# The modulation product of a two-block kernel, on TensorE or on VectorE, and its latent projections in quarters

## The reference

```python
def second_block(x, c, ctx, c_ctx, w_mod, b_mod, ...):
    mod   = silu(c) @ w_mod + b_mod              # w_mod: 1024 x 6144
    sh1, sc1, g1, sh2, sc2, g2 = split(mod, 6)
    mod_c = silu(c_ctx) @ w_mod + b_mod          # only csh1, csc1 are used
    h  = rmsnorm(x, norm1_g) * (1 + sc1) + sh1
    hc = rmsnorm(ctx, norm1_g) * (1 + csc1) + csh1
    qkv, z, ba, sc_p, fn_u = split(h @ w_in)     # latent projections
    ...                                          # the same for hc
    o_ctx, o_lat = bidirectional_gated_delta(context, latent)
    y_dn = (rmsnorm(o_lat) * silu(z)) @ w_dn_out
    y_sc = (sb * conv(sc * sx)) @ w_sc_out
    y_fn = real(fft2(fn_u)) @ w_fn_out
    gates = sigmoid(h @ w_gate + b_gate)         # three of 1024 columns
    merged = gates[0] * y_dn + gates[1] * y_sc + gates[2] * y_fn
    x = x + g1 * (merged @ w_o)
    x = x + g2 * swiglu(rmsnorm(x, norm2_g) * (1 + sc2) + sh2)
    return rmsnorm(x, final_g)
```

## Time and profile before

| | us |
|---|---|
| median of three runs | 1279.43 |
| profiled execution, span from first to last instruction | 1276.8 |
| runs, lowest and highest | 1279.11, 1280.48 |
| TensorE busy | 1239.6 |
| VectorE busy | 861.0 |
| ScalarE busy | 642.9 |
| GpSimd busy | 96.6 |

### The profile page before, as it was taken

One profiled execution on the slowest core, in us unless ns is written; L12 is line 12 of the kernel. 1 busy time (PEld: TensorE's weight loads), 2 busy tenths in 40 slices (PEclk: granted clock), 3 DMA queues, 4 the chain that ended last, 5 costly groups with the idle time before them and its releaser, 6 DMA issues.

```text
span 1276.8 us, 20625 instructions
## 1 busy us (share of the span) xinstructions
PE 1239.6 (97%) x8338; PEld 1101.1 (86%) x8338; DVE 861.0 (67%) x1278; ACT 642.9 (50%) x983; POOL 96.6 (8%) x84
## 2 busy tenths in 40 slices
PE   8999999999999999999999999999899999999997
PEld 7989778888999889999999989986789998888885
DVE  6877656667879278665546866785476776666665
ACT  6574424435666366554463665552345555344443
POOL 0420000000024020000000000324100000000000
PEclk9999999999999999999999999999999999999999
DMA  9635876555673454454443655537115566555530
GB/s 325 205 106 175 282 259 206 195 181 191 223 218 100 136 162 131 136 163 135 163 133 126 195 175 158 173 100 249 48 67 169 194 217 219 203 188 196 198 133 33
DMA packets 164620, 219.15 MB, mean 172 GB/s; under 512 B 5456, under 2 KB 135342, under 8 KB 164398
## 3 DMA queue, kind: packets, MB, share of 16 engines
q1 hardware_dynamic: 162802, 214.45, 51.4%
q10 hardware_dynamic: 1724, 3.39, 0.7%
HBM read 215.99 MB, written 1.05 MB: 170 GB/s over the span
## 4 chain that ended last, share of the span: by engine, by line
PE 85%; DVE 8%; ACT 3%; DVEq 2%; issue 1%; ACTq 1%; DMA 0%
PE bank L555 16%; PE bank L557 16%; PE bank L556 16%; PE bank L599 15%; PE bank L601 7%; DVE w_lo L546 2%; PE bank L645 2%; PE bank L911 1%; PE bank L899 1%; PE bank L1486 1%; PE bank L1465 1%; PE bank L928 1%; DVE arena L1275 1%; PE bank L1689 1%; PE bank L919 1%
## 5 line engine op out<-in xcount | busy, mean ns | idle before, releaser
L546 DVE TENSOR_TENSOR w_lo<-w_raw,w_hi 128x1024 fp32r<-128x1024 f32 (+1 forms) x350 | 421.7, 1249 | 64.8 <-ACT w_hi L537 54.9
L537 ACT ACTIVATE w_hi<-w_raw 128x1024 fp32r<-128x1024 f32 (+1 forms) x350 | 348.8, 1040 | 121.0 <-PE bank L557 62.7
L599 PE MATMUL bank<-act_parts,w_hi 128*128 128x512 f32 x800 | 283.1, 397 | 2.1 <-DVE act_parts L2259 0.7
L555 PE MATMUL bank<-act_parts,w_hi 128*128 128x256 f32 x944 | 271.0, 287 | 6.6 <-DVE act_parts L2344 3.6
L556 PE MATMUL bank<-act_parts,w_hi 128*128 128x256 f32 x944 | 267.0, 283 | 0.0
L557 PE MATMUL bank<-act_parts,w_lo 128*128 128x256 f32 x944 | 266.9, 283 | 0.0
L601 PE MATMUL bank<-act_parts,w_lo 128*128 128x256 f32 x800 | 224.0, 280 | 0.0
L555 PEld LDWEIGHTS bank<-act_parts,w_hi 128*128 128x128 f32 x944 | 180.8, 192 | 14.5 <-issue 8.9
L599 PEld LDWEIGHTS bank<-act_parts,w_hi 128*128 128x128 f32 x800 | 150.1, 188 | 43.5 <-issue 5.8
L556 PEld LDWEIGHTS bank<-act_parts,w_hi 128*128 128x128 f32 x944 | 181.0, 192 | 0.3 <-issue 0.2
L557 PEld LDWEIGHTS bank<-act_parts,w_lo 128*128 128x128 f32 x944 | 181.0, 192 | 0.0
(11 more groups left out here) (340 smaller groups left out, 1583.1 us busy)
## 6 DMA issues: line engine op xcount, KB each, us to landing
w_raw<-in_w_in SPq DMA_DIRECT2D x39, 1024.0 KB, 6.0
w_raw<-in_w_up SPq DMA_DIRECT2D x32, 1024.0 KB, 5.6
w_raw<-in_w_down SPq DMA_DIRECT2D x32, 1024.0 KB, 5.4
w_raw<-in_w_mod SPq DMA_DIRECT2D x24, 1024.0 KB, 5.4
w_raw<-in_w_ffn_in SPq DMA_DIRECT2D x22, 1024.0 KB, 5.2
w_raw<-in_w_gate SPq DMA_DIRECT2D x20, 1024.0 KB, 5.2
w_raw<-in_w_ffn_out SPq DMA_DIRECT2D x11, 1024.0 KB, 5.9
w_raw<-in_w_out SPq DMA_DIRECT2D x8, 1024.0 KB, 5.1
```

Source lines behind the costliest of these rows:

```text
L537: nc.scalar.activation(whi[:, slot, 0:n], raw[:, st.slot(name), n * half:n * (half + 1)], ACT.Copy).then_inc(hi_ready, 1)
L546: nc.vector.tensor_tensor(wlo[:, slot, 0:n], raw[:, st.slot(name), n * half:n * (half + 1)], whi[:, slot, 0:n].bitcast(F32), ALU.subtract) ...
L555: nc.tensor.matmul(o, ahi, bhi, start=start, stop=False, skip_group_check=True)
L599: nc.tensor.matmul(pair(two_banks[m]), whi[:, slot, at:at + P], xall[:, f, :, :], start=f == 0, stop=False, skip_group_check=True)
```

## The change

The modulation chunk is now 256 rows by 1024 columns; six groups of 1024 columns have four parts each, the same 24 MB. VectorE scales each weight row by the condition's value on that partition and adds it to an accumulator of 128 x 1024: two halves a part, for one condition (groups 2 to 5) or two (0 and 1). Behind the fourth part TensorE sums the accumulator over its partitions with a matrix of ones, ScalarE copies the rows, TensorE turns them and VectorE adds the bias. The slot of a part comes free when VectorE has read it. The parts of groups 0 and 1 stand in layer 0's FFN, 2 and 3 in layer 1's, 4 in the gates, 5 in the SwiGLU.

The latent projections are issued in four units of 12 matmuls: 8 units at `ba`, 8 at `norm`, 3 at each T, and 12 in the levels. Their order changes (the Fourier inputs first, z last), `final_norm` comes in the first T with it, the last copy stands behind the levels, and the fills have two banks of their own. The up products of layer 0 stay wide.

```diff
-        "lat": dict(ba=2, norm=4, T0=1, T1=1, T2=1, T3=1, end=1)}
+        "lat": dict(ba=8, norm=8, T0=3, T1=3, T2=3, T3=3, x0=1, z1=1, x1=1, z2=1, x2=1, z3=1, x3=1, z4=1, x4=1, z5=1,
+                    x5=1, z6=1, end=1)}
-LAT_FILL = ["z0", "z1"] + [f"sc{c}" for c in range(6)] + ["fn0", "fn1"]
-LAT_EXTRA = {"P": [("mod", 8)], "x0": [("mod", 9), ("modr", 4)], "z1": [("modc", 4)],
...
+LAT_FILL = ["fn0", "fn1"] + [f"sc{c}" for c in range(6)] + ["z0", "z1"]
+LAT_EXTRA = {"z5": [("fold", 0)], "z6": [("fold", 1)]}
...
+mod_group(0, 0, (16, 18, 21, 24), 27, 28)
+mod_group(0, 1, (30, 33, 36, 39), 43, 44)
+mod_group(1, 2, (19, 21, 23, 25), 27, 28)
+mod_group(1, 3, (30, 32, 34, 36), 37, 38)
+GATE_MODS = {5: 0, 7: 1, 9: 2, 12: 3}
+GATE_SUMMED, GATE_TURNED = 14, 15
+FFN_MODS = {1: 0, 2: 1, 3: 2, 4: 3}
+FFN_SUMMED, FFN_TURNED = 6, 7
...
-        mod_cond = sb("silu_c_cols", [P, KT, 32])
+        mod_cond = sb("silu_c_cols", [P, KT, 2])
+        mod_acc = sb("mod_terms", [P, D])
...
-                mm.then_inc(pieces_done, 1)
+                    if m == ms - 1:
+                        mm.then_inc(pieces_done, 1)
+                    yield
...
+            def mod_rows_sum(g, take):
+
+                b = banks.claim(pe, f"mod{g}", take())
+                pe.wait_ge(S("mod_done"), MOD_PARTS * (g + 1))
+                for c, acc in enumerate((mod_acc[:, :], ctx_acc) if g < CTX_GROUPS else (mod_acc[:, :],)):
+                    for i in range(4):
+                        mm = nc.tensor.matmul(ps[b][32 * i:32 * (i + 1), T * c:T * (c + 1)], ones[:, 0:32],
+                                              acc[:, T * i:T * (i + 1)], start=True, stop=True, skip_group_check=True)
+                mm.then_inc(S("mod_summed"), 1)
...
+            def mod_terms(i):
+
+                g, r = divmod(i, MOD_PARTS)
+                name = ("mod", i)
+                if r == 0 and g:
+                    dve.wait_ge(S("mod_summed"), g)
+                dve.wait_ge(landed[st.slot(name)], st.loads(name))
+                sums = (mod_acc[:, :], ctx_acc) if g < CTX_GROUPS else (mod_acc[:, :],)
+                for half in range(2):
+                    k, w = 2 * r + half, raw[:, st.slot(name), D * half:D * (half + 1)]
+                    for j, acc in enumerate(sums):
+                        if k == 0:
+                            v.tensor_scalar(acc, w, mod_cond[:, k, j:j + 1], None, ALU.mult)
+                        else:
+                            v.scalar_tensor_tensor(acc, w, mod_cond[:, k, j:j + 1], acc, ALU.mult, ALU.add)
+                    if half == 0:
+                        dve.drain()
+                dve.drain().then_inc(S("mod_done"), 1)
...
+                elif before in st.mods:
+                    sp.wait_ge(S("mod_done"), st.mods[before] + 1)
```

More of the change, by code:

```diff
@@ L58 @@
 PW = CH // 2
[L60 to L61 removed]
+MOD_GROUPS = 6
+MOD_ROWS = 256
+MOD_PARTS = D // MOD_ROWS
+CTX_GROUPS = 2
 LAYER_CHUNKS = 52
@@ L271, in attention_order, with mod_group @@
             V(3) + T(4, 5) + conv[2] + ctx[3] + V(4, 5) + conv[3])
-def mod(*chunks):
-    return [("mod", i) for i in chunks]
 FFN_EXTRA = ({}, {})
[L280 to L283, removed]
+def mod_group(layer, g, steps, summed, turned):
+    for r, at in enumerate(steps):
+        FFN_EXTRA[layer].setdefault(at, []).append(("mod", MOD_PARTS * g + r))
+    FFN_EXTRA[layer].setdefault(summed, []).append(("modr", g))
+    FFN_EXTRA[layer].setdefault(turned, []).append(("modc", g))
+mod_group(0, 0, (16, 18, 21, 24), 27, 28)
[6 more added lines that the diff above has]
+FFN_SUMMED, FFN_TURNED = 6, 7
 ATT = [attention_order(layer) for layer in range(DEPTH)]
@@ L562, in project, with project_parts @@
         def project(pe, name, out_tile, kts, act_hi, act_lo, wait_act=None, first=True, last=True):
+            for _ in project_parts(pe, name, out_tile, kts, act_hi, act_lo, wait_act, first, last):
+                pass
+        def project_parts(pe, name, out_tile, kts, act_hi, act_lo, wait_act=None, first=True, last=True):
             n = st.width(name)
@@ L1031, in act_delta @@
                     nc.scalar.activation(rs, rs, ACT.Exp, scale=-0.5).then_inc(S("dn_rs"), 1)
-                fill("norm", 1)
+                fill("norm", FILL[part]["norm"] // (4 if lat else 2))
             fill("norm")
@@ L1113, in act_delta @@
                 fill(f"t{lv}")
+            fill("end")
             for g in range(4):
@@ L1191, in dve_delta @@
                     S("lat_qn" if lat and i < 2 else "dn_kn"), 1)
-                fill("norm", 1)
+                fill("norm", FILL[part]["norm"] // nq)
             fill("norm")
@@ L1545, in first_input @@
                 def first_input(f):
-                    if layer and f == 4:
-                        mod_chunk(12, low)
-                        mod_chunk(13, low)
                     wait("n1_act", f + 1, KT)
@@ L1746, in _, with gate_mods @@
                 full(mm, b)
+            def gate_mods():
+                if l - GATES_AT == GATE_SUMMED:
+                    mod_rows_sum(4, take)
+                if l - GATES_AT == GATE_TURNED:
+                    mod_columns(4)
             for n in range(3):
@@ L2111, in lat_fill @@
             def lat_fill():
-                i = left[0]
+                i, part = divmod(left[0], UNITS)
                 left[0] += 1
-                if i < len(LAT_FILL):
-                    nxt(n_tiles + i)
-                if i and i - 1 not in settled:
+                if i < len(LAT_FILL) and part % 2 == 0:
+                    split_hi(act, ("post", n_tiles + i + 1), (part // 2,))
+                if i and part == 0 and i - 1 not in settled:
                     lat_copy(i - 1)
@@ L2627, in lat_fill @@
             def lat_fill():
-                i = left[0]
+                i, part = divmod(left[0], UNITS)
                 left[0] += 1
-                nxt(n_tiles + i)
+                if part % 2 == 0:
+                    split_lo(dve, ("post", n_tiles + i + 1), (part // 2,))
+                if part:
+                    return
                 if i == 4:
```

223 lines of the change are left out of this document (96 added, 127 removed).

## The result

The changed kernel took 1321.05 us, the median of four runs (1320.04 to 1323.68); the kernel before 1279.95 beside it. The ratio is 1.0322, 95% interval 1.0308 to 1.0337: slower by 41 us, where 12.7 were forecast. The direction was right, the size was off by a factor of three, and the time lies far outside the range.

The account below looks back on a forecast made before the run. TensorE was taken to bound the kernel, with VectorE costing only where a split comes late. The terms summed to +12.7 us on the 1276.8 span, 1289.5, plus 2.6 to the median: 1292.2 us, range 1277 to 1303.

Parts of the forecast that it names:

- part 1: Layer 0's FFN, groups 0 and 1: VectorE's parts delay splits, stalls 23.5, sums and turns 2.8, less 13.4 of modulation: +12.9 us.
- part 2: Modulation chunks TensorE did while waiting: removal brings nothing, only uncovered turns go; layer 1's start -0.9 us.
- part 3: Layer 1's FFN, groups 2 and 3: parts fit VectorE's idle time; sums, turns and 0.3 of stall: +2.0 us.
- latent inputs: First latent input: the hidden modulation chunks' removal brings nothing, their uncovered turn goes: -0.35 us.
- part 4: Latent delta: norm stage -11.8, T stage -1.6, levels with projection quarters +8.4: -5.0 us.
- part 5: Gates, group 4: stalls of 2.2 at the fourth part, 0.65, 0.3 and 0, sum and turn 0.8: +4.0 us.
- w_o: w_o's first chunk: the hidden modulation chunks' removal brings nothing, their uncovered turn goes: -0.36 us.
- part 6: Last FFN, group 5: no stall, +0.8 for sum and turn, -0.35 for the turn that goes: +0.45 us.
- rival C: Three 4.3 us TensorE stalls drop the clock to 1.2 GHz for the next product, 5.6 each: +17, 1309; chance 0.06.
- the stage longer by 13: Sign in layer 0's FFN: the stage from step 14 to 45 grows by 13 us.
- a granted clock below 1 behind a stall: Sign that the forecast is wrong: the clock drops behind a TensorE stall; expected chance of that case 0.06.

Follow-up runs that it names:

- fit_only: Changed kernel with spare matmuls fitted into TensorE's waits, none at the first gate products or in the context's delta: 1309.1 us, ratio 1.0238.
- warm_hidden: Changed kernel with 13 spare matmuls in each of the four places where modulation chunks stood ahead of a TensorE wait: 1320.1 us, ratio 1.0307.
- bank_fix: Changed kernel with group 3's sum of columns ahead of VectorE's split, and group 5's turn and sum a product earlier: 1314.1 us, ratio 1.0271.
- whole_proj: Changed kernel with the ten latent projections whole again at their old places, none in the levels: 1320.7 us, ratio 1.0313.

## Why the prediction was wrong, point by point

The terms, forecast and measured on the two profiled executions (their spans differ by 45.1, as this one was the slowest of its four runs; the medians by 41.1):

| term | forecast | measured | of it slow clock |
|---|---|---|---|
| part 1, layer 0's FFN | +12.9 | +22.9 | 7.8 |
| part 2, layer 1's start | -0.9 | +2.0, with layer 0's gate | 3.3 |
| part 3, layer 1's FFN | +2.0 | +5.6 | 0 here |
| latent inputs | -0.35 | +0.4 | 1.7 |
| part 4, latent delta | -5.0 | -4.1 | about 3 |
| part 5, gates, to w_o's first chunk | +4.0 | +8.6 | 3.3 |
| w_o | -0.36 | -0.5 | 0 |
| part 6, last FFN | +0.45 | +8.1 | 3.3 |
| ahead of layer 0's FFN | 0 | +1.1 | 0 |
| last norm, end | 0 | +0.9 | not counted |

The last column is an estimate: half of each slow stretch, less what of it was idle. It sums to 22, while fit_only, with 41.0 of the 47.8 us of slow stretches gone, gained 12.0 in the medians (15.6 between the profiled executions). So take the column as an upper bound; why a slow stretch costs less than TensorE loses in it is open.

- **Part 1's mechanism was right to the step.** Stalls forecast and measured: 0.6 and 0.6, 2.6 and 2.4, 1.2 and 1.2, 1.0 and 0.7, then 4.3 and 4.47 to 4.48 three times, 1.3 + 0.55 and 1.83 or 1.5 + 0.3; 23.5 in sum against 22.8 (at step 30 0.5 and 0.3 for a forecast of 1.0). One outer bound was added up wrong, 38.2 for 37.2; nothing hangs on it. The terms' price held (1.28 each, 1.2 start to start; a first term 0.75), and so did the sums (8 matmuls and 2 turns as forecast). Missing were the clock and refill, 2 to 3 us by my estimate: a down product behind a stall took 5.7 from start to start at full clock, where an undisturbed one takes 5.48.
- **The step that failed is the clock.** The sum put what TensorE does after a wait at nothing; rival C had it with a chance of 0.06, only behind the three stalls of 4.3, at +17. I had looked at the one wait of 2.77 at the end of the kernel before and taken it as a bound below which nothing happens; right behind it the kernel ends, so it could not show what comes after. The trace of the kernel before does show the lower clock, at both of its ends. TensorE's last matmul ends at 1272.85, and the granted clock falls at 1275.86, in this row (columns as above):

```profile
1274.00:1276.00 2.00, 0.00 (x0) 0.00 (x0) 0.00 (x0) 0.00 (x0) 0.00 (x0) 0.97 0.99 383
```

  At the start, behind a first wait of 3.83 us (longer than the 2.77 that the prediction calls the longest) and one of 1.06, TensorE's matmuls of 256 columns take 0.41 us, as in the slow stretches, and 0.28 from 16.41 on:

```profile
16.02 0.41 PE L555 MATMUL bank<-side_hi,w_hi 128*128 128x256 f32 x1
16.24 0.34 PE L556 MATMUL bank<-side_lo,w_hi 128*128 128x256 f32 x1
16.41 0.28 PE L557 MATMUL bank<-side_hi,w_lo 128*128 128x256 f32 x1
```

  The page's 9 in the first slice hides this, because the record of the clock begins only at 16.3 us; "the granted clock stayed 1.00 in every slice" was a misreading. Behind each of the three stalls the loss was 1.6 to 2.9 and not 5.6, but slow stretches stood behind much shorter waits as well, at nine other places. By fit_only all this is worth 12 of the 28 us between forecast and measurement.
- **"So their removal brings nothing" (part 2) was right about the wait and wrong about the work.** The hidden chunks had cost nothing and kept TensorE from being idle. That removing them costs something is read from the slow stretches behind three of the four places; warm_hidden didn't settle it. Of all the terms of the sum this is the one whose sign a reader would least suspect.
- **Part 6 and part 3: a bank.** I costed the sum and the turn by their own durations and said nothing of the bank that they hold. The ring has four, a wide product takes two, and the bank of the modulation comes up again at the second claim. By bank_fix this is worth 7 us.
- **Part 4 came out at its number for another reason than its working gave it.** whole_proj shows that the quarters brought nothing. What the stage gained is then, as far as the rows say, the eight modulation chunks of 1.06 and their turns that left it, less some 3 us of slow clock; no run took these apart.
- **Part 5**: the fourth part's stall was 2.73 for a forecast of 2.2, with 6.8 us at 1.2 GHz about it.

Of the signs to look for nearly all came: the stalls at 23, 35 and 41, those of 1 to 2 at 26 and 38, the first T at 815.6 in the old time, levels of 9 us, a stall of 2.7 behind the fourth part. One did not, the stage longer by 13 (it was 22.9), and the one named as "wrong would be: a granted clock below 1 behind a stall" came too. The range ended at 1303 and left out rival C's 1309 by choice; to hold what was measured, C would have had to stand behind the shorter waits as well.

## What to carry to other kernels

An engine at 97% is worth keeping busy: before moving work off it, list the waits that the work was filling and those that its new place makes, and price what the engine does after each, not only the wait. Where a part is put on a second engine in program order, its length must fit the idle stretch at that place; the same work in halves, all at the better places, cost 28 us less. A new use of a ring of banks is a wait too: count the claims until its bank comes up, and see where the instruction that frees it stands in the other engine's order.

## What the runs showed of the hardware

Over the 17 profiled executions of this case, from 100 us on and without the last 15, I counted TensorE's idle times and how many had a stretch at 1.2 GHz begin in them or just behind:

| idle time of TensorE | of these | with a slow stretch |
|---|---|---|
| 0.5 to 1.2 us | 174 | 0 |
| 1.2 to 1.7 | 60 | 10 |
| 1.7 to 2.2 | 29 | 20 |
| 2.2 to 3.2 | 74 | 46 |
| over 3.2 | 24 | 24 |

In the middle the length alone doesn't decide: the wait of 2.3 us in the context's delta has one behind it in seven of these kernels and none in the changed one, though in most nothing near it was edited. With one trace of each kernel it is open whether such a shift comes from an edit further up or differs from one execution to the next. Executions of one kernel do differ: 1314.8 to 1322.4 in warm_hidden, against 1279.2 to 1281.4 for the kernel before beside it. The kernel before is not free of it either: over all sittings its 29 runs at a mean granted clock of 0.998 have a median of 1278.9 us, its 11 at 0.995 one of 1280.9.

The granted clock was 0.50 or 1.00 and nothing between. The Trainium skill, "TensorE: Matmul & The Clock Gate", "What's actually happening", says the same: two states, the throttled one as the default, released by activity. The traces agree: matmuls of 256 columns take 0.41 us at the start of the kernel before and 0.28 from 16.41 on, and each later slow stretch ends while TensorE works.

A term on VectorE costs by its form: 128x1024 fp32 took 0.75 us as tensor_scalar and 1.28 as scalar_tensor_tensor. The Trainium skill, "VectorE: DVE Perf Modes", "The perf-mode tier table (the rule you actually need)", has fp32 tensor_scalar at twice the rate of tensor_tensor. The trace agrees roughly: 0.66 us from start to start for tensor_scalar against 1.16 for a split, which is a tensor_tensor of the same size. It also shows that the accumulating form, 1.20 from start to start, runs like the second.
